# Block attention: the second residual quarter by a trip through DRAM, and the first two tiles taken in turns

## The reference, cut to what matters

```python
for i in range(DEPTH):                      # DEPTH = 2
    hn = rms_norm_2(h, norm_g[i])
    if i % 2 == 0:
        h = h + short_conv_mixer(hn, conv_w_in[j], conv_w[j], conv_w_out[j])
    else:
        h = h + moba_mixer(hn, attn_w_in[j], q_norm_g[j], k_norm_g[j], attn_w_out[j])
```

## Time and profile before

| | |
|---|---|
| median of three runs | 899.53 us |
| the profiled execution | 899.7 us |
| its span | 897.9 us |
| PE busy | 892.8 us (99%) |
| DVE busy | 653.1 us (73%) |
| ACT busy | 506.9 us (56%) |
| DMA, mean rate | 209 GB/s |
| raw fetch, median to landing | 4.6 us |

### The profile page before, as it was taken

The page is one execution under the profiler, slowest core; times in us unless marked ns, Lnnn a source line. Parts: engine busy times, 40 slices in busy tenths (PEclk is TensorE's granted clock), DMA queues, the critical chain, the costliest instruction groups (busy, mean ns, idle before and its releaser), DMA issues.

```text
span 897.9 us, 12240 instructions
## 1 busy us (share of the span) xinstructions
PE 892.8 (99%) x4364; PEld 738.6 (82%) x4364; DVE 653.1 (73%) x985; ACT 506.9 (56%) x820; POOL 69.4 (8%) x88
## 2 busy tenths in 40 slices
PE   9999999999999999999999999999999999999998
PEld 8988888888888888778888888888888888887777
DVE  5985478777745688997787777645778997779763
ACT  6756455444444666788664444434665555577681
POOL 0000100000000303211000000000010000215100
PEclk9999999999999999999999999999999999999999
DMA  7674558867755656434387766746567876566621
GB/s 258 205 236 136 179 186 293 283 235 240 247 202 187 226 187 221 143 116 141 127 277 268 244 243 237 253 137 235 197 244 239 286 248 211 191 212 226 222 87 47
DMA packets 76988, 187.47 MB, mean 209 GB/s; under 512 B 6852, under 2 KB 31812, under 8 KB 76936
## 3 DMA queue, kind: packets, MB, share of 16 engines
q1 hardware_dynamic: 75480, 182.99, 59.9%
q0 software_dynamic: 1024, 3.15, 1.0%
q10 hardware_dynamic: 432, 0.66, 0.2%
HBM read 171.83 MB, written 14.94 MB: 208 GB/s over the span
## 4 chain that ended last, share of the span: by engine, by line
PE 98%; DMA 1%; DVE 1%; ACT 0%; issue 0%; DVEq 0%; ACTq 0%
PE bank L1818 86%; PE bank L1856 3%; PE bank L1871 1%; PE bank L2131 1%; PE bank L2157 1%; PE bank L2241 1%; PE bank L2271 1%; DMA h_land<-gate_blocks 1%; PE bank L2142 0%; PE bank L1914 0%; PE bank L1978 0%; PE bank L2227 0%; PE bank L2026 0%; PE bank L2030 0%; PE bank L2251 0%; PE bank L2117 0%
## 5 line engine op out<-in xcount | busy, mean ns | idle before, releaser
L699 ACT ACTIVATE whi<-raw 128x1024 fp32r<-128x1024 f32 x295 | 306.3, 1060 | 181.2 <-DMA raw<-stream_dram 106.2
L1108 DVE TENSOR_TENSOR wlo<-raw,whi 128x1024 fp32r<-128x1024 f32 x295 | 347.9, 1214 | 57.1 <-ACT whi L699 56.7
L1818 PE MATMUL bank<-whi,x_hi 128*128 128x512 f32 x560 | 152.5, 394 | 0.0
L1818 PE MATMUL bank<-wlo,x_hi 128*128 128x512 f32 x560 | 149.9, 390 | 0.0
L1818 PE MATMUL bank<-whi,x_lo 128*128 128x512 f32 x560 | 149.8, 389 | 0.0
L1818 PEld LDWEIGHTS bank<-wlo,x_hi 128*128 128x128 f32 x560 | 105.2, 188 | 22.1
L1818 PEld LDWEIGHTS bank<-whi,x_lo 128*128 128x128 f32 x560 | 105.2, 188 | 21.9
L1818 PEld LDWEIGHTS bank<-whi,x_hi 128*128 128x128 f32 x560 | 103.6, 188 | 22.1 <-issue 1.8
L1818 PE MATMUL bank<-whi,y_hi 128*128 128x512 f32 x396 | 107.8, 394 | 0.6 <-ACT ple_gate L895 0.5
L1818 PE MATMUL bank<-wlo,y_hi 128*128 128x512 f32 x396 | 106.0, 390 | 0.0
L1818 PE MATMUL bank<-whi,y_lo 128*128 128x512 f32 x396 | 106.0, 390 | 0.0
(11 more groups left out here) (252 smaller groups left out, 898.7 us busy)
## 6 DMA issues: line engine op xcount, KB each, us to landing
raw<-stream_dram SPq DMA_DIRECT2D x295, 512.0 KB, 4.6
ffn_blocks<-ffn_blk SPq DMA_DIRECT2D x22, 256.0 KB, 2.0
ffn_land<-ffn_blocks SPq DMA_DIRECT2D x22, 256.0 KB, 4.0
second_blocks<-h_blk SPq DMA_DIRECT2D x8, 256.0 KB, 2.0
h_land<-second_blocks SPq DMA_DIRECT2D x8, 256.0 KB, 2.8
cv_blocks<-cv_blk SPq DMA_DIRECT2D x7, 256.0 KB, 5.0
cv_land<-cv_blocks SPq DMA_DIRECT2D x7, 256.0 KB, 3.1
h_blocks<-h_blk SPq DMA_DIRECT2D x3, 512.0 KB, 6.3
```

The lines of the kernel that those rows point to most:

```text
L699: A(whi[:, u % RING, :], raw[:, u % RAW, :], ACT.Copy).then_inc(sem("w_hi"), 1)
L1108: V.tensor_tensor(wlo[:, u % RING, :], raw[:, u % RAW, :], whi[:, u % RING, :].bitcast(F32), ALU.subtract).then_inc(sem("w_lo"), 1)
L1818: last = T.matmul(bank[pair + t][:, :], lhs[a][:, kt, t * P:(t + 1) * P], w[:, u % RING, kk * NW:(kk + 1) * NW], start=part != 1 and k == ...
```

## The change

- Quarter 1 of the block attention's input goes by the trip as well (the piece "mb h1"). PE makes 4 transposes instead of 8, into one bank.
- DVE makes the block transposes of that quarter right after the left half's `residual`, and ACT and DVE take it from `h_land`.
- SP does that trip at unit M+5, ahead of the fetches of M+5, M+6 and M+7: one write, then one read.
- The first two tiles now go by turns: quarter 0 of the first tile, 0 of the second, then quarter 1 of both, then quarters 2 and 3 as before. So quarter 1 is first used at M+2 and no longer at M+1, and the second tile's banks are first used at M+1 and no longer at M+2.
- "mb h1" and "mb q1" share slot 1, so SP reads "mb q1" only when the low part of "mb h1" is done.
- All trips of all stages are numbered in one list (`PIECES`) and go through one function, `trips`, and one DRAM tensor. From the second use of a slot on, DVE waits for the slot's last write before it transposes (not in the `gate` pieces).

```diff
+PIECES = ("mix0 q0", "mix0 q1", "gate0 t0", "gate0 t1", "mix1 q0", "mix1 q1", "gate1 t0", "gate1 t1",
+          "cv q0", "cv q1", "mb h1", "mb q0", "mb q1")
+MB_PAIR_ORDER = ((0, 0), (1, 0), (0, 1), (1, 1), (0, 2), (0, 3), (1, 2), (1, 3))
...
+            def trips(at, *names):
+
                 fetch(done, at)
+                for name in names:
+                    n, q = piece(name), slot(name)
+                    sp.wait_ge(sem("g_blk"), n + 1)
+                    sp.dma_start(s_dram[n], sblk[:, q, :]).then_inc(sem(f"g_out{q}"), 16)
+                for name in names:
+                    n, q = piece(name), slot(name)
+                    if name == "mb q1":
+                        sp.wait_ge(sem("g_lhs"), piece("mb h1") + 1)
+                    sp.wait_ge(sem(f"g_out{q}"), 16 * turn(name))
+                    sp.dma_start(sland[:, q, :, :], s_dram[n].rearrange("q n -> (q n)")
                                  .rearrange("(i p w) -> p i w", i=P // B, p=P)).then_inc(sem(f"g_land{q}"), 16)
...
-            done = second_blocks(5, MB_IN)
+            done = trips(END[MB_IN] + 5, "mb h1")
+            done = trips(END[MB_IN] + 8, "mb q0", "mb q1")
...
                 split_to(END[first] + 2 + AHEAD)
-                lhs_hi(dst, norm_gain(j), (4, 5))
+                lhs_hi(dst, norm_gain(j), (4,))
                 squares(j, 0)
                 split_to(END[first + 1] + 1 + AHEAD)
+                pair_hi(j, dst, "mb h1", 2)
                 squares(j, 1)
-                second_hi(j, dst, 5, END[first + 1])
+                second_hi(j, dst, "mb", END[first + 1])
...
+            def pair_blk(name, news, kt0, first):
+
+                if turn(name) > 1:
+                    dve.wait_ge(sem(f"g_out{slot(name)}"), 16 * (turn(name) - 1))
...
             residual(CV_OUT, 0, END[CV_OUT] + 5)
+            pair_blk("mb h1", 24, 2, True)
             split_to(END[CV_OUT] + 6 + AHEAD)
-            lhs_lo(X, norm_gain(7), (4, 5))
+            lhs_lo(X, norm_gain(7), (4,))
             residual(CV_OUT + 1, 1)
-            second_blk(26)
-            second_lo(7, X, 5, END[MB_IN])
+            second_blk("mb", 26)
+            pair_lo(7, X, "mb h1", 2)
+            second_lo(7, X, "mb", END[MB_IN])
...
-            product(CV_OUT + 1, Y, None, only=2, at=out_at + 6, hooks=[(2, lambda: got.extend(h_T(0, 7)))])
+            product(CV_OUT + 1, Y, None, only=2, at=out_at + 6, hooks=[(2, first_quarter)])
...
-            first_tiles(MB_IN, X, "mb_in", list(got) + second_need(5), mb_beside)
+            first_tiles(MB_IN, X, "mb_in", list(got) + [piece_need("mb h1")] + second_need("mb"), mb_beside)
```

More of the change, by code:

```diff
@@ L77, with piece, slot, turn @@
 LAST = ((0, 0, NW), (1, 0, NW // 2), (1, NW // 2, NW))
+PIECES = ("mix0 q0", "mix0 q1", "gate0 t0", "gate0 t1", "mix1 q0", "mix1 q1", "gate1 t0", "gate1 t1",
+          "cv q0", "cv q1", "mb h1", "mb q0", "mb q1")
+MB_PAIR_ORDER = ((0, 0), (1, 0), (0, 1), (1, 1), (0, 2), (0, 3), (1, 2), (1, 3))
 PAIR_ORDER = ((0, 0), (0, 1), (1, 0), (1, 1), (0, 2), (0, 3), (1, 2), (1, 3))
+def piece(name):
+    return PIECES.index(name)
+def slot(name):
+    return int(name[-1])
+def turn(name):
+    return sum(slot(other) == slot(name) for other in PIECES[:piece(name) + 1])
 def done_at(tile):
@@ L430, in _ @@
             for tile in PAIRED:
-                for n, (t, k) in enumerate(PAIR_ORDER):
+                for n, (t, k) in enumerate(MB_PAIR_ORDER if tile == MB_IN else PAIR_ORDER):
                     SOURCE[END[tile] + n] = END[tile] + (KT // 2) * t + k
@@ L529, in _ @@
                 done = END[out_tile]
[L530 removed]
+                done = trips(END[tin] + 8, f"mix{n} q0", f"mix{n} q1")
                 fetch(done, done_at(tin) + 10)
@@ L714, in norm_gain, with pair_hi @@
                 return lambda kt: cols[:, C_NORM + j * KT + kt:C_NORM + j * KT + kt + 1]
+            def pair_hi(j, dst, name, kt0):
+                q = slot(name)
+                act.wait_ge(sem(f"g_land{q}"), 16 * turn(name))
+                for k in range(2):
+                    A(dst[0][:, kt0 + k, :].rearrange("p (t i b) -> p t i b", t=TT, b=B),
+                      sland[:, q, :, :].rearrange("p i (k t b) -> p k t i b", k=2, t=TT)[:, k], ACT.Copy,
+                      scale=norm_gain(j)(kt0 + k)).then_inc(sem("g_hi"), 1)
             def mixer_lhs(j, dst, out):
@@ L722, in mixer_lhs, with second_hi @@
                 squares(j, 1)
-                second_hi(j, dst, 2 * (j - 1) // 3, END[out + 4])
-            def second_hi(j, dst, r, base):
+                second_hi(j, dst, f"mix{(j - 1) // 3}", END[out + 4])
+            def second_hi(j, dst, name, base):
                 split_to(base + 8)
                 for q in range(2):
[L729 to L734, removed]
+                    pair_hi(j, dst, f"{name} q{q}", 4 + 2 * q)
             def squares(j, half):
@@ L1152, in second_lo @@
-            def second_lo(j, dst, r, base):
+            def pair_blk(name, news, kt0, first):
+                if turn(name) > 1:
+                    dve.wait_ge(sem(f"g_out{slot(name)}"), 16 * (turn(name) - 1))
+                for t in range(TT):
+                    if first:
+                        dve.wait_ge(sem("h_new"), news + t + 1)
+                    at = slice(kt0 * P, (kt0 + 2) * P)
+                    last = V.transpose(sblk[:, slot(name), :].rearrange("p (f k t b) -> p t f k b", f=P // B, k=2, t=TT)[:, t],
+                                       h[:, t, at].rearrange("p (k b f) -> p f k b", b=B, f=P // B))
+                last.then_inc(sem("g_blk"), 1)
@@ new lines, in pair_lo @@
+            def pair_lo(j, dst, name, kt0):
+                n = piece(name)
+                for k in range(2):
+                    kt = kt0 + k
+                    dve.wait_ge(sem("g_hi"), 2 * n + k + 1)
+                    for t in range(TT):
+                        at = slice(t * P, (t + 1) * P)
+                        part = sland[:, slot(name), :, :].rearrange("p i (k t b) -> p k t i b", k=2, t=TT)[:, k, t]
+                        last = V.scalar_tensor_tensor(dst[1][:, kt, at].rearrange("p (i b) -> p i b", b=B), part,
+                                                      norm_gain(j)(kt),
+                                                      dst[0][:, kt, at].bitcast(F32).rearrange("p (i b) -> p i b", b=B),
+                                                      ALU.mult, ALU.subtract)
+                last.then_inc(sem("g_lhs"), 1)
@@ L1154, in second_lo, with second_blk @@
+            def second_blk(name, news):
+                for q in range(2):
+                    pair_blk(f"{name} q{q}", news, 4 + 2 * q, q == 0)
+            def second_lo(j, dst, name, base):
                 split_to(base + 8)
                 for q in range(2):
[L1156 to L1165, removed]
@@ L2099, in ffn @@
                 product(tple + 2, src, "ple_sig")
-                half1 += [("g_lhs", 2 * (2 * n + 1) + k + 1, ("g_hi", 4 * (2 * n + 1) + k + 3)) for k in range(2)]
+                r = piece(f"gate{n} t0")
+                half1 += [("g_lhs", r + k + 1, ("g_hi", 2 * r + k + 3)) for k in range(2)]
                 product(tple + 3, PT, "ple_gated")
```

76 lines of the change are left out of this document (25 added, 51 removed).

## The result

The changed kernel takes 901.18 us (median of 21 runs, 899.59 to 903.69), the kernel before 899.12 us beside it (21 runs, 897.96 to 900.74). The medians lie 2.1 us apart. The ratio on record is 1.0026, 95% interval [1.0021, 1.0032]: slower, clear of the noise, by about a quarter of a per cent. The profiled execution took 902.72 us with a span of 900.6 us.

A forecast was written before the change was run, and what follows sets the result against it. PE's work was taken to bound the kernel. Removing four transposes gave -0.44 us and every other step 0, so 899.53 - 0.44 = 899.1 us, range 898.6 to 900.2.

The forecast's parts named there:

- What bounds the kernel: Whole kernel: PE's work sets the time, busy 892.8 of 897.9 us, with its clock already at the upper level.
- The transposes, 0.44 us: Before the block attention: four of PE's eight transposes of `h` go, gaining 0.44 us if no wait replaces them.
- The Trainium skill's 275 ns for one transpose: Rule for PE's removed transposes: four would be worth 1.10 us, giving 898.43; the prediction did not adopt it.
- Step 1: DVE's block transposes of quarter 1 after the left half's `residual`: write issued at 756.34, delayed `wlo` parts still free.
- Step 2: Quarter 1's write to DRAM, with M+4 still in flight: taken to land after 2.6 us, possible span 2.0 to 5.9.
- W: Landing time of quarter 1's write: taken as 2.6 us, with no PE wait at M+2 while below 3.9.
- case B: Rival: quarter 1's trip comes a little late, PE waits 0 to 2.0 us at M+2; 899.9 us, chance 0.12.
- near 4: Quarter 1's write by the skill's high-load HBM access time: landing near 4 us, a 0.1 us wait, total 899.2.
- Step 3: SP's queue, held by quarter 1's write: M+6 goes out late and lands 4.8 us after its issue.
- Steps 4 to 9: Block attention's start: the read, ACT's and DVE's parts, banks, later read and squares all come in time, costing 0.
- step 4's margin: ACT finishes quarter 1's high part, behind M+6's, 1.3 us before PE wants it at M+2.
- C: Rival: PE waits at M+2 because ACT holds quarter 1 behind M+6, whose fetch SP holds; 901.5 us, chance 0.05.

The follow-up runs named there:

- experiment 1: Changed kernel, but SP issues the fetches of M+5 and M+6 between quarter 1's write and its read: 898.81 us, ratio 0.9998 to the kernel before.
- experiment 9: Changed kernel, but SP fetches M+7 only behind the writes of quarters 2 and 3: 899.10 us, ratio 1.0004 to the kernel before.
- experiments 3 and 4: First: changed kernel without quarter 1's trip and the turns (plumbing alone), 899.17 us. Second: kernel before with only the turns added, 899.13 us.

## Why the prediction was wrong

The forecast was 899.1 us (898.6 to 900.2) with no wait at M+2. Measured were 901.18 us and waits of 0.5 to 2.3 us there. The steps that failed are 2 and 3, the two landing times. A term for the clock and one for the time outside the span were missing.

- **What bounds the kernel.** Right. PE bound it before and after, and its list of waits carried the answer. What was missing is that PE's clock is part of the bound: "no time is to be had from the clock" looked only at gaining. A wait of 2.26 us cost 1.73 us more through it, and no case had a term for that.
- **The transposes, 0.44 us.** Right on the path: the chain of experiment 1 has them as `755.89 0.44 PE bank L1900 x4`. But 0.34 us came back outside the span in every kernel with the trip, so a tenth of a microsecond is what could be gained. No version was told apart from the kernel before.
- **The Trainium skill's 275 ns for one transpose** (TensorE: Matmul & The Clock Gate, Part 4: PE-mode transpose), 1.10 us for four, did not hold as a step on the path here: four took 0.44 us, as the rows had said.
- **Step 1**, the write at 756.34 in the calendar of before: right. The changed kernel's profile ran 1.3 us early there (0.9 from its start, the rest mainly from the gate stage), and the write came 2.38 us behind the `residual`'s start (755.02 - 752.64), where 2.39 was predicted.
- **Step 2 is the first that failed: W = 2.6.** It took 4.1, 3.8 and 3.4 us in the three profiles of the changed kernel. I argued it down to the midpoint of a write with nothing in flight and the fastest among units. All seven of those had taken 3.1 or more, and case B said so. The argument for going lower was that only 1.2 us of M+4's transfer was left. In the three profiles 2.1, 1.4 and 1.6 us of it were left, and in experiment 9, with only 0.4 us left, the write still took 3.1. The Trainium skill (DMA: Bandwidth & Descriptors, Latency and other measured facts) has an HBM access at 2 us at high load, from which the prediction had the estimate "near 4"; the three profiles agree with that number better than with my 2.6, and no run shows that the load of the memory is the reason.
- **Step 3 is the second: M+6 lands in 4.8 us.** It took 6.9, 6.5 and 5.9. The rows I took the earlier trace rows are the first two units behind two reads. In the hold the fetches pile up and go out 0.5 us apart, so M+6 is under way together with the read, M+5 and M+7, and from 763.67 on with the write of quarter 2. Without the hold (experiment 1) it took 4.7, with the hold and without M+7 (experiment 9) 5.0. The trace of before had a nearer row than the mean of two: M+6 is the second of its bunch, and the second there took 5.2. The slowest row was that of the unit fetched between 769.9 and 770.5, the third behind the reads, which took

```profile
DMA to landing us min/median/max: 6.0/6.0/6.0
```

  With W = 4 and 6.0 (a row chosen with the result in hand) the steps give a wait of 1.3 us, and with the slow ends (4.1, 6.9) the measured 2.3. The form of the sum was right to 0.1 us in four profiles. Its two terms were mis-sized, 0.8 to 1.5 and 1.1 to 2.1 us.
- **Steps 4 to 9.** Right but for step 4's margin of 1.3 us, which rests on steps 2 and 3: the read was never the limit (2.8 us), DVE's low part and the banks at M+1 brought no wait, and experiments 3 and 4 show the plumbing and the turns to be free.
- **The rivals.** C was the mechanism to the letter and had 0.05. That its 901.5 us lies near the measured 901.18 is luck: it was priced with W = 5.9 and no clock. In truth W was smaller, the units were slower, and in part of the runs the clock made up the rest. B has the waits of the runs without a fall of the clock, though not by the W of 3.9 and more that it asked for. The two landings were late together: 3.4 with 5.9, 3.8 with 6.5, 4.1 with 6.9, 4.3 with 7.0. Why is not shown; I had kept one at its middle while varying the other, up to 5.2.

## What to carry to other kernels

When a wait is put into a queue that also carries the steady stream, the stream's fetches come out of it in a bunch and were slower each here (5.9 to 7.0 us instead of 4.8), so price the held fetches with the slowest row of a bunch, and add that to the hold itself. The first repair to try is to issue what is ready behind the write before waiting for it, or to let the consumer take the piece before the units it holds up; either alone took away the 2 us. And where TensorE is busy all the time, a wait of about 2 us may cost nearly twice its length, as 2.26 us did here with 1.73 us more, because the clock can fall with it.

## What the runs showed of the hardware

- The granted clock went from the upper to the lower level just behind a wait of 2.26 us (1.73 us lost) and within one of 5.21 us (2.56 us lost), each after more than 100 us in which PE had not waited. It did not with waits of 1.60 and 0.51 us.
- The 256 KB write of quarter 1 took 3.1 to 4.3 us with the end of one or two 512 KB fetches still under way. The writes of quarters 2 and 3, issued among M+6 and M+7, took 5.3 and 4.8 us in the changed kernel's first profile, and 2.0 us in the kernel before, where nothing was in flight.
- Behind the read of quarter 1, a 512 KB fetch took 3.6 to 3.9 us as the first of three issued 0.5 us apart, 5.9 to 7.0 us as the second, and 5.0 us as the second of two.
- Device time less span agrees within about 0.1 us between the runs of one kernel and is 0.34 us larger on average in every kernel that makes the additional trip; one more write alone does not do it.
